# Softmax normalisation folded into the transposes of two attention stages

## The chip, the cores and the metric

The kernel runs on one core of one Trainium2 chip. The metric is the device time of one execution in microseconds (us). The engines named below are TensorE (PE in the profile; PEld is its weight load), VectorE (DVE), ScalarE (ACT), GpSimd (POOL) and SyncE (SP), which issues most of the transfers.

## The reference

The program is a chain of layers on one sequence of 512 positions with 1024 features, in float32: a convolution layer, a linear recurrence, feed-forward layers, and two attention layers. Only the attentions are touched. The first has 4 heads and a causal mask:

```
s = jnp.einsum('bqhd,bkhd->bhqk', qn, k_nope) + jnp.einsum('bqhr,bkr->bhqk', qr, k_rope)
s = s.astype(jnp.float32) * scale
s = jnp.where(k_idx[None, :] <= q_idx[:, None], s, -jnp.inf)
p = jax.nn.softmax(s, axis=-1).astype(v.dtype)
return jnp.einsum('bhqk,bkhd->bqhd', p, v)
```

The second has 8 heads and looks at selected keys only, at most 128 for each query:

```
logits = jnp.einsum('bthd,btkhd->bthk', q_b, k_sel).astype(jnp.float32) * (dh ** -0.5)
logits = jnp.where(valid[:, :, None, :], logits, -jnp.inf)
p = jax.nn.softmax(logits, axis=-1).astype(v.dtype)
return jnp.einsum('bthk,btkhd->bthd', p, v_sel)
```

## The kernel before, in words

Every engine has its own program, and semaphores tie them together; the order on each engine is written out by hand. Queries are worked in four blocks of 128, and query block qb sees (qb+1)*128 keys, so a matrix of probabilities is 128 x 128, 256, 384 or 512.

**First attention** (`attention_pe`, `attention_act`, `attention_dve`): 16 units, one for each of 4 heads and 4 query blocks. For a unit TensorE makes the scores (two instructions of the program, scores and mask, L2342 and L2344). VectorE takes the row maximum (L2407) and scales it (L2409). ScalarE computes exp into SBUF and the row sums beside it (L2391). VectorE takes the reciprocal of the sums (L2418) and multiplies the probabilities by it in place (L2420), which raises `at_norm`. TensorE waits for `at_norm`, then transposes the probabilities, one 128 x 128 block at a time, into PSUM bank 3 of `gp` (L2369). ScalarE copies the result to SBUF (L2384), which raises `at_pt`, and TensorE multiplies by the values (L2351). The loop on TensorE is score(i+2), values(i-1), transposes of i, and then, behind four of the units, a tile of another branch's product (L2563). VectorE weighs that tile (L2951), which lets GpSimd add it up (L2518).

**Second attention** (`pairs_pe`, `pairs_act`, `pairs_dve`): 16 pairs of heads; i//4 is the query block and i%4 the pair. The steps are the same with other lines: scores and mask L3339 and L3342, maximum L3591 and L3592, exp L3564, reciprocal L3599, multiplication L3602 (one for each head), transposes `turn(i, h)` (L3353), copy L3574 or L3579, values L3364. For query blocks 0 and 1 both heads are transposed before one copy; for blocks 2 and 3 the order on TensorE is turn(i, 0), values(i-1), turn(i, 1), and each head has its own copy into SBUF. Beside the pairs TensorE makes products of a convolution (L3305), VectorE selects keys (L3673 to L3698) and ScalarE and GpSimd normalise the convolution (L3505, L3517, L3173 to L3181). The output projection (L3399) comes behind all of it.

Both attentions alternate two buffers of probabilities and two of transposed ones. ScalarE's exp(i) waits until the transposes of i-2 are done.

Of the kernel before, what the change touches and what calls it, by code (L numbers as in the profile page):

```python
# [22 lines left out]
ALU = mybir.AluOpType  # L23
AX = mybir.AxisListType

P = 128
# [185 lines left out]
def build(nc, d, out):  # L212
    ctx = ExitStack()
    with ctx:
# [38 lines left out]
        arena = sb("arena", [P, NT, S])  # L253
# [7 lines left out]
        root = sb("root", [P, S])  # L261
        par = sb("par", [P, NPAR])
        cst = sb("cst", [P, NCST])
        gp = ctx.enter_context(nc.psum_tensor("gp", [P, BANKS, S], F32))
        aux = ctx.enter_context(nc.psum_tensor("aux", [P, BANKS, S], F32))
# [8 lines left out]
        ident, ones, bones = const("ident"), const("ones"), const("bones")  # L274
# [2060 lines left out]
        def attention_pe(pe, A, beside=None):  # L2335
            def score(i):
                u, n = A.units[i], A.u0 + i
                if n >= A.banks:
                    pe.wait_ge(at_exp, n - A.banks + 1)
                if u.chosen:  # L2340
                    pe.wait_ge(sel_ready, u.chosen)
                nc.tensor.matmul(gp[:, n % A.banks, 0:u.nk], u.q, u.k, start=True, stop=False, skip_group_check=True)  # L2342
                lo, m = u.mask
                nc.tensor.matmul(gp[:, n % A.banks, lo:u.nk], A.eye, m, start=False, stop=True,  # L2344
                                 skip_group_check=True).then_inc(at_score, 1)

            def values(i):
                u, n = A.units[i], A.u0 + i
                pe.wait_ge(at_pt, n + 1)
                for b in range(u.nk // P):  # L2350
                    last = nc.tensor.matmul(u.out, u.v(b), A.pt(n)[:, b * P:(b + 1) * P],  # L2351
                                            start=(b == 0), stop=(b == u.nk // P - 1))
                last.then_inc(at_pv, 1)

            score(0)
            score(1)
            if beside:
                beside(-1)
            for i, u in enumerate(A.units):
                n = A.u0 + i  # L2360
                if i + 2 < len(A.units):
                    score(i + 2)
                if i:
                    values(i - 1)
                pe.wait_ge(at_norm, n + 1)
                if n:
                    pe.wait_ge(at_pt, n)
                for b in range(u.nk // P):
                    last = nc.tensor.transpose(gp[:, 3, b * P:(b + 1) * P], A.p(n)[:, b * P:(b + 1) * P], ident)  # L2369
                last.then_inc(at_tr, 1)  # L2370
                if beside:
                    beside(i)
            values(len(A.units) - 1)

        def stat(n, i):
            return root[:, 4 * (n % 2) + i:4 * (n % 2) + i + 1]

        def attention_act(act, A, beside=None):
            def copy(i):
# [23 lines left out]
        def attention_dve(dve, v, A, beside=None):  # L2403
            def maximum(i):
                u, n = A.units[i], A.u0 + i
                dve.wait_ge(at_score, n + 1)
                v(nc.vector.tensor_reduce(stat(n, 0), gp[:, n % A.banks, 0:u.nk], AX.X, ALU.max))  # L2407
                if u.root is None:
                    nc.vector.tensor_scalar(stat(n, 1), stat(n, 0), -A.scale, None, ALU.mult).then_inc(at_max, 1)  # L2409
                else:  # L2410
                    nc.vector.tensor_scalar(stat(n, 1), stat(n, 0), u.root, -1.0, ALU.mult, ALU.mult).then_inc(at_max, 1)

            maximum(0)
            maximum(1)
            for i, u in enumerate(A.units):
                n = A.u0 + i
                dve.wait_ge(at_exp, n + 1)
                v(nc.vector.reciprocal(stat(n, 3), stat(n, 2)))  # L2418
                p = A.p(n)[:, 0:u.nk]
                nc.vector.tensor_scalar(p, p, stat(n, 3), None, ALU.mult).then_inc(at_norm, 1)  # L2420
                if i + 2 < len(A.units):
                    maximum(i + 2)
                if beside:
                    beside(i)
# [655 lines left out]
        score_banks = lambda i: slice(2 * (i % 2), 2 * (i % 2) + 2)  # L3080
        chances = lambda i: 8 + 2 * (i % 2)
        turned = lambda i: (42, 46)[i % 2]
        pair_stat = lambda i, kind: root[:, 8 * (i % 2) + 2 * kind:8 * (i % 2) + 2 * kind + 2]
        head_root = lambda i, n=2, h=0: HST[:, qb_of(i) * 2 * AH + 2 * hp_of(i) + h:qb_of(i) * 2 * AH + 2 * hp_of(i) + h + n]
        head_out = lambda i, h: aux[half(h), qb_of(i) % 2, hp_of(i) * P:(hp_of(i) + 1) * P]
# [244 lines left out]
        def pairs_pe(pe, beside):  # L3330
            def score(i):
                qb, hp, nk = qb_of(i), hp_of(i), nk_of(i)
                lo, chosen = (64, mask3[:, 0, CHUNKED]) if qb == 0 else (0, sel3[:, qb - 1, 0:nk])
                if i >= 2:
                    pe.wait_ge(at_exp, PAIR0 + 2 * (i - 1))
                if qb:
                    pe.wait_ge(sel_ready, qb)
                for h in range(2):
                    nc.tensor.matmul(gp[:, 2 * (i % 2) + h, 0:nk], arena[half(h), dQ + hp, q_cols(qb)],  # L3339
                                     arena[half(h), dK + hp, 0:nk], start=True, stop=False, skip_group_check=True)  # L3340
                for h in range(2):
                    last = nc.tensor.matmul(gp[:, 2 * (i % 2) + h, lo:nk], mask3[:, 0, EYE], chosen, start=False, stop=True,  # L3342
                                            skip_group_check=True)
                last.then_inc(at_score, 1)

            def turn(i, h):
                qb, nk = qb_of(i), nk_of(i)
                at0 = h * nk if qb < 2 else 0
                pe.wait_ge(at_norm, PAIR0 + 2 * i + h + 1)
                if i:  # L3350
                    pe.wait_ge(at_pt, PAIR0 + 2 * i + (0 if qb < 2 else h))
                for b in range(qb + 1):
                    last = nc.tensor.transpose(aux[:, 2, at0 + b * P:at0 + (b + 1) * P],  # L3353
                                               arena[:, chances(i) + h, b * P:(b + 1) * P], ident)
                last.then_inc(at_tr, 1)

            def values(i):
                qb, hp = qb_of(i), hp_of(i)
                pe.wait_ge(at_pt, PAIR0 + 2 * i + 2)
                if qb >= 2 and hp == 0:  # L3360
                    pe.wait_ge(dsa_root, USED + qb - 1)
                for b in range(qb + 1):
                    for h in range(2):
                        last = nc.tensor.matmul(head_out(i, h), arena[:, dV + b, (2 * hp + h) * HD:(2 * hp + h + 1) * HD],  # L3364
                                                arena[:, turned(i) + h, b * P:(b + 1) * P], start=(b == 0), stop=(b == qb),
                                                skip_group_check=True)
                last.then_inc(at_pv, 1)

            score(0)
            score(1)  # L3370
            beside(-1)
            for i in range(PAIRS):
                if i + 2 < PAIRS:
                    score(i + 2)
                turn(i, 0)
                if qb_of(i) < 2:
                    turn(i, 1)
                if i:
                    values(i - 1)
                if qb_of(i) >= 2:  # L3380
                    turn(i, 1)
                beside(i)
            values(PAIRS - 1)
# [204 lines left out]
        def pairs_dve(dve, v, beside):  # L3588
            def maximum(i):
                dve.wait_ge(at_score, PAIR0 + i + 1)  # L3590
                v(nc.vector.tensor_reduce(pair_stat(i, 0), gp[:, score_banks(i), 0:nk_of(i)], AX.X, ALU.max))  # L3591
                nc.vector.scalar_tensor_tensor(out=pair_stat(i, 1), in0=pair_stat(i, 0), scalar=-1.0, in1=head_root(i),  # L3592
                                               op0=ALU.mult, op1=ALU.mult).then_inc(at_max, 1)

            maximum(0)
            maximum(1)
            for i in range(PAIRS):
                dve.wait_ge(at_exp, PAIR0 + 2 * i + 2)
                v(nc.vector.reciprocal(pair_stat(i, 3), pair_stat(i, 2)))  # L3599
                for h in range(2):  # L3600
                    p = arena[:, chances(i) + h, 0:nk_of(i)]
                    nc.vector.tensor_scalar(p, p, pair_stat(i, 3)[:, h:h + 1], None, ALU.mult).then_inc(at_norm, 1)  # L3602
                if i + 2 < PAIRS:
                    maximum(i + 2)
                beside(i)
# [562 lines left out]
```

## Time and profile before

| | us |
|---|---|
| three runs | 3144.32, 3146.17, 3157.05 |
| median | 3146.17 |
| the profiled execution | 3143.76 |
| its span in the trace | 3141.9 |
| TensorE busy, of the span | 3067.1 (98%) |
| VectorE busy | 1595.1 (51%) |
| ScalarE busy | 1177.2 (37%) |
| GpSimd busy | 1276.0 (41%) |

Of the span, the first attention takes from 1975.7 to 2017 us, the second from 2641 to 2717 us. A busy TensorE is not a TensorE at its peak: its instructions are pipelined, and the duration of one includes the time that its result needs to arrive. What one more instruction of a row costs is read from rows that differ in their count.

### The profile page before, as it was taken

To read this page: it belongs to the slowest core of one execution; us is meant where nothing else is said; L and a number is where in the kernel's file an instruction comes from. 1 tells how busy PE (TensorE), PEld (TensorE's weight loads), DVE (VectorE), ACT (ScalarE), POOL (GpSimd) and SP (SyncE) were. 2 spreads that over 40 slices of the span, in tenths; PEclk is the share of its full clock that TensorE was granted. 3 is DMA by queue.
4 is the path that set the end of the run, shared out by engine and by line. 5 is a ranking of instruction groups with operands and counts; after the bars stand their busy time and mean duration, and the time that the engine had idled before them with its cause. 6 is when DMAs were issued, how large, how long until landed. Compare 5 with 4: busy or idle time off the path is not lost.

```text
span 3141.9 us, 58978 instructions
## 1 busy us (share of the span) xinstructions
PE 3067.1 (98%) x23898; PEld 2381.9 (76%) x23898; DVE 1595.1 (51%) x2426; ACT 1177.2 (37%) x1623; POOL 1276.0 (41%) x661
## 2 busy tenths in 40 slices
PE   9999999999999999999999999899999999899999
PEld 6758888868688886888887877678887673458887
DVE  6655555067465554666564641664141776544140
ACT  6413444223444443444334323442232434532221
POOL 4333444434244331444454434344444364224443
PEclk9999999999999999999999999999999999999999
DMA  4212333323100001444553322123333222023333
GB/s 141 80 53 76 99 94 100 103 78 94 48 3 3 3 3 49 141 150 144 188 202 109 97 78 87 39 83 101 94 98 96 67 72 64 13 82 95 100 94 101
DMA packets 74757, 268.64 MB, mean 86 GB/s; under 512 B 8863, under 2 KB 8874, under 8 KB 74384
## 3 DMA queue, kind: packets, MB, share of 16 engines
q1 hardware_dynamic: 73680, 262.53, 26.9%
q0 software_dynamic: 896, 3.52, 0.3%
q8 instruction: 135, 2.21, 0.3%
q14 instruction: 46, 0.38, 0.0%
HBM read 261.71 MB, written 2.10 MB: 84 GB/s over the span
## 4 chain that ended last, share of the span: by engine, by line
PE 88%; issue 6%; DVE 3%; ACT 2%; POOL 1%; DMA 0%; SPq 0%; DVEq 0%; POOLq 0%; ACTq 0%
PE gp L385 66%; PE gp L1344 5%; PE aux L1344 1%; POOL w_low L360 1%; PE gp L2563 1%; PE gp L3282 1%; PE gp L1364 1%; PE aux L1339 1%; PE aux L1480 1%; PE gp L1414 1%; PE aux L3226 1%; PE aux L1443 1%; PE aux L3305 0%; PE aux L808 0%; PE gp L860 0%
## 5 line engine op out<-in xcount | busy, mean ns | idle before, releaser
L360 POOL TENSOR_TENSOR w_low<-ring,w_high 128x1024 fp32r<-128x1024 f32 x413 | 1000.7, 2425 | 1447.1 <-ACT w_high L330 1446.8
L330 ACT ACTIVATE w_high<-ring 128x1024 fp32r<-128x1024 f32 x413 | 437.0, 1059 | 969.6 <-DMA ring<-in_weights 967.3
L385 PE MATMUL gp<-ffn_h,w_high 128*128 128x512 f32 x2432 | 750.3, 390 | 3.0 <-POOL w_low L360 1.3
L385 PEld LDWEIGHTS gp<-ffn_h,w_high 128*128 128x128 f32 x2432 | 455.8, 188 | 101.8 <-issue 3.9
L385 PE MATMUL gp<-ffn_h,w_low 128*128 128x512 f32 x1216 | 473.1, 389 | 0.0
L385 PE MATMUL gp<-ffn_high,w_high 128*128 128x512 f32 x928 | 361.0, 389 | 0.0
L385 PE MATMUL gp<-ffn_low,w_high 128*128 128x512 f32 x864 | 336.1, 389 | 0.0
L385 PE MATMUL gp<-ffn_high,w_low 128*128 128x512 f32 x864 | 336.1, 389 | 0.0
L385 PE MATMUL gp<-in_h,w_high 128*128 128x512 f32 x896 | 278.9, 392 | 0.0
L385 PEld LDWEIGHTS gp<-ffn_h,w_low 128*128 128x128 f32 x1216 | 228.2, 188 | 47.6
L2463 DVE TENSOR_TENSOR arena<-arena 128x512 f32<-128x512 f32 x64 | 102.0, 1593 | 216.8 <-ACTq L164 213.5
L385 PEld LDWEIGHTS gp<-ffn_high,w_high 128*128 128x128 f32 x928 | 174.2, 188 | 36.3
L385 PEld LDWEIGHTS gp<-in_h,w_high 128*128 128x128 f32 x896 | 168.6, 188 | 37.4 <-issue 2.7
L385 PEld LDWEIGHTS gp<-ffn_low,w_high 128*128 128x128 f32 x864 | 162.2, 188 | 33.8
L385 PEld LDWEIGHTS gp<-ffn_high,w_low 128*128 128x128 f32 x864 | 162.2, 188 | 33.4
L385 PE MATMUL gp<-in_h,w_low 128*128 128x512 f32 x448 | 174.6, 390 | 0.0
L385 PE MATMUL gp<-hyena_high,w_high 128*128 128x512 f32 x304 | 121.3, 399 | 1.3 <-POOL w_low L360 1.1
L1173 ACT ACTIVATE arena<-gp,par 128x512 f32<-128x512 f32 x88 | 68.6, 779 | 139.3 <-DVEq L164 139.3
L385 PE MATMUL gp<-hyena_high,w_low 128*128 128x512 f32 x304 | 118.5, 390 | 0.0
L3618 DVE SCALAR_TENSOR_TENSOR X<-gp,par,X 128x512 f32<-128x512 f32 x24 | 18.0, 751 | 186.3 <-PE gp L385 155.9
L2281 DVE TENSOR_TENSOR gp<-gp,arena 128x512 f32<-128x512 f32 x48 | 33.4, 699 | 155.9 <-PE gp L385 154.7
L1205 DVE TENSOR_TENSOR gp<-gp,root 128x512 f32<-128x512 f32 x88 | 61.5, 699 | 81.8 <-PE gp L385 66.2
(598 smaller groups left out, 5052.2 us busy)
## 6 DMA issues: line engine op xcount, KB each, us to landing
ring<-in_weights SPq DMA_DIRECT2D x437, 512.0 KB, 3.6
H<-in_ada SPq DMA_DIRECT2D x48, 512.0 KB, 4.4
arena<-arena SPq DMA_DIRECT2D x32, 67.5 KB, 2.0
X<-in_x SPq DMA_DIRECT2D x4, 512.0 KB, 6.3
out_x<-X SPq DMA_DIRECT2D x8, 256.0 KB, 4.4
arena<-in_sm POOLq DMA_DIRECT2D x1, 1024.0 KB, 5.0
cst<-in_cst SPq DMA_DIRECT2D x1, 756.0 KB, 10.9
arena<-in_hy_f_w POOLq DMA_DIRECT2D x1, 512.0 KB, 5.2
```

The costliest lines, as they stand in the source:

```text
L330: nc.scalar.activation(w_high[:, slab % RING, :], ring[:, slab % RING, :], ACT.Copy).then_inc(high_ready, 1)
L360: nc.gpsimd.tensor_tensor(w_low[:, slab % RING, :], ring[:, slab % RING, :], w_high[:, slab % RING, :], ALU.subtract).then_inc(low_ready, 1)
L385: last = nc.tensor.matmul(gp[:, t.bank, :], wt[:, slab % RING, w], x(k), start=(k == 0 and q == 0), stop=(k == sum(kt) - 1 and q == 2))
L1173: nc.scalar.activation(tmp, z, ACT.Identity, scale=ff_cols(layer, t, 1), bias=pcol("ff_conv_b", layer * 2 * F1T + t.idx)).then_inc(aff_rea ...
L1205: v.go(nc.vector.tensor_tensor(z, z, root[:], ALU.mult))
L1339: last = nc.tensor.matmul(out[h], lhsT[h], rhs[h], start=start, stop=True, skip_group_check=True)
L1344: return nc.tensor.matmul(out[HEADS[cols]], lhsT[HEADS[rows]], rhs[HEADS[rows]], start=start, stop=True, skip_group_check=True)
L1364: last = nc.tensor.matmul(dst, w[:, k, :], X[:, k, :], start=(k == 0), stop=(k == DT - 1))
L1414: last = nc.tensor.matmul(gp[:, t.bank, :], ring[half, slot, i * P:(i + 1) * P], src, start=True, stop=True)
L1443: last = nc.tensor.transpose(aux[:, bank + d, j * P:(j + 1) * P], src(d, j), ident)
L2281: nc.vector.tensor_tensor(z, z, COMB, ALU.mult).then_inc(in2_scaled, 1)
L2463: v(nc.vector.tensor_tensor(f, f, f, ALU.mult))
```

## The change

The probabilities keep the scale that exp gives them. VectorE multiplies the 128 x 128 identity by the reciprocals instead, which makes a diagonal matrix, and TensorE's transpose (the probabilities as the stationary operand, the identity as the moving one) becomes an ordinary float32 product of the same stationary operand with that diagonal matrix. So the result in PSUM is transposed and scaled in one. The diagonal matrices lie in `root` (first attention) and in arena tile 44 (second attention), two buffers for each in turn. The number and the order of the program's instructions on every engine, and all waits, stay as they are.

```diff
@@ attention_pe
                 for b in range(u.nk // P):
-                    last = nc.tensor.transpose(gp[:, 3, b * P:(b + 1) * P], A.p(n)[:, b * P:(b + 1) * P], ident)
+                    last = nc.tensor.matmul(gp[:, 3, b * P:(b + 1) * P], A.p(n)[:, b * P:(b + 1) * P], weight_of(n),
+                                            start=True, stop=True)
...
+        def weight_of(n):
+            return root[:, P * (1 + n % 2):P * (2 + n % 2)]
@@ attention_dve
                 v(nc.vector.reciprocal(stat(n, 3), stat(n, 2)))
-                p = A.p(n)[:, 0:u.nk]
-                nc.vector.tensor_scalar(p, p, stat(n, 3), None, ALU.mult).then_inc(at_norm, 1)
+                nc.vector.tensor_scalar(weight_of(n), ident, stat(n, 3), None, ALU.mult).then_inc(at_norm, 1)
@@ second attention
+        weights_of = lambda i, h: arena[:, 44, (2 * (i % 2) + h) * P:(2 * (i % 2) + h + 1) * P]
...
-                    last = nc.tensor.transpose(aux[:, 2, at0 + b * P:at0 + (b + 1) * P],
-                                               arena[:, chances(i) + h, b * P:(b + 1) * P], ident)
+                    last = nc.tensor.matmul(aux[:, 2, at0 + b * P:at0 + (b + 1) * P],
+                                            arena[:, chances(i) + h, b * P:(b + 1) * P], weights_of(i, h), start=True,
+                                            stop=True)
...
                 for h in range(2):
-                    p = arena[:, chances(i) + h, 0:nk_of(i)]
-                    nc.vector.tensor_scalar(p, p, pair_stat(i, 3)[:, h:h + 1], None, ALU.mult).then_inc(at_norm, 1)
+                    nc.vector.tensor_scalar(weights_of(i, h), ident, pair_stat(i, 3)[:, h:h + 1], None,
+                                            ALU.mult).then_inc(at_norm, 1)
```

## Rows read from the trace of the kernel before

**Rows 1.** The page: TensorE's busy time, and the chain by engine.

```profile
PE 3067.1 (98%) x23898; PEld 2381.9 (76%) x23898; DVE 1595.1 (51%) x2426; ACT 1177.2 (37%) x1623; POOL 1276.0 (41%) x661
PE 88%; issue 6%; DVE 3%; ACT 2%; POOL 1%; DMA 0%; SPq 0%; DVEq 0%; POOLq 0%; ACTq 0%
```

**Rows 2.** Chain of work, first attention: start us, length us, what.

```profile
1977.96 0.33 PE gp L2369
...
2013.96 0.67 PE gp L2369 x4
...
2017.81 7.33 PE gp L2563 x31
```

**Rows 3.** Timeline, end of the second attention: start us, length us, instruction [idle before].

```profile
2714.16 0.60 ACT L3579 ACTIVATE arena<-aux 128x512 f32<-128x512 f32 x1 [0.87 <-PE aux L3353]
2715.71 0.60 ACT L3579 ACTIVATE arena<-aux 128x512 f32<-128x512 f32 x1 [0.95 <-PE aux L3353]
2716.36 1.09 PE L3364 MATMUL aux<-arena 128*64 128x128 f32 x16 [0.69 <-ACT arena L3579]
```

**Rows 4.** Timeline, transposes of 1 and of 3 blocks, first attention.

```profile
1998.81 0.33 PE L2369 MATMUL gp<-cst,arena 128*128 128x128 f32 x1
...
2002.98 0.55 PE L2369 MATMUL gp<-cst,arena 128*128 128x128 f32 x3
```

**Rows 5.** Timeline: four transposes, then four ordinary float32 products of 128 columns.

```profile
2712.03 0.63 PE L3353 MATMUL aux<-cst,arena 128*128 128x128 f32 x4 [1.59 <-ACT arena L3579]
2712.49 1.06 PE L3388 MATMUL aux<-arena,cst 128*128 128x128 f32 x8
```

**Rows 6.** Timeline, VectorE's multiplications undisturbed: pairs of 128, 256, 384, 512 columns.

```profile
2661.62 0.48 DVE L3602 TENSOR_SCALAR arena<-arena,root 128x128 f32<-128x128 f32 x2
2666.04 0.62 DVE L3602 TENSOR_SCALAR arena<-arena,root 128x256 f32<-128x256 f32 x2
2685.35 0.75 DVE L3602 TENSOR_SCALAR arena<-arena,root 128x384 f32<-128x384 f32 x2
2707.99 0.88 DVE L3602 TENSOR_SCALAR arena<-arena,root 128x512 f32<-128x512 f32 x2
```

**Rows 7.** Timeline: VectorE's multiplication beside a GpSimd addition, and what follows.

```profile
1997.26 1.27 POOL L2518 TENSOR_TENSOR H<-H,arena 128x512 f32<-128x512 f32 x1 [5.67 <-DVEq L164]
1997.41 1.21 DVE L2420 TENSOR_SCALAR arena<-arena,root 128x128 f32<-128x128 f32 x1
...
2003.88 1.26 POOL L2518 TENSOR_TENSOR H<-H,arena 128x512 f32<-128x512 f32 x1 [5.35 <-DVEq L164]
2004.03 1.40 DVE L2420 TENSOR_SCALAR arena<-arena,root 128x512 f32<-128x512 f32 x1
...
2005.49 0.66 PE L2369 MATMUL gp<-cst,arena 128*128 128x128 f32 x4 [0.51 <-DVE arena L2420]
...
2012.09 1.81 DVE L2420 TENSOR_SCALAR arena<-arena,root 128x512 f32<-128x512 f32 x1
```

**Rows 8.** Timeline, second attention: a wait for VectorE, and one for ScalarE.

```profile
2661.96 0.69 PE L3353 MATMUL aux<-cst,arena 128*128 128x128 f32 x2 [2.73 <-DVE arena L3602]
...
2694.87 0.52 PE L3353 MATMUL aux<-cst,arena 128*128 128x128 f32 x3 [0.54 <-ACT arena L3579]
```

**Rows 9.** Stretches of the second attention: us, busy of each engine, PEclk, DMA.

```profile
2648.00:2652.00 4.00, 4.00 (x24) 0.89 (x22) 3.83 (x10) 1.87 (x6) 2.54 (x2) 0.57 0.00 0
...
2663.00:2666.00 3.00, 3.00 (x24) 0.76 (x24) 2.86 (x6) 1.25 (x5) 0.00 (x0) 0.62 0.00 0
...
2670.00:2717.00 47.00, 40.83 (x322) 24.34 (x316) 37.66 (x76) 30.31 (x75) 16.80 (x12) 1.00 0.00 1
```

**Rows 10.** Timeline: groups of convolution products at the lower and at the full clock.

```profile
2647.88 4.48 PE L3305 MATMUL aux<-arena 128*32 128x512 f32 x24
...
2653.70 2.78 PE L3305 MATMUL aux<-arena 128*32 128x512 f32 x24
...
2663.21 3.78 PE L3305 MATMUL aux<-arena 128*32 128x512 f32 x24
```

## The prediction

> **What bounds the kernel now.** I read the page first: TensorE is busy 98% of the span and carries 88% of the chain that ended last [rows 1]. So the question for each attention is whether TensorE, or something that TensorE waits for, sets its end. The chain of work answers it for the first attention: it runs from unit to unit through TensorE, with VectorE's multiplication in it where that was late, and its last piece there goes straight on into the products of the next branch [rows 2]. Nothing behind the attention would absorb a delay. In that stretch the chain holds 12 of the 16 groups of transposes, with 1, 3, 4, 2, 3, 4, 1, 2, 4, 1, 2 and 4 blocks, 31 of the 40 blocks; the shown rows are the first and the last of the 12.
>
> For the second attention the printed chain breaks off at a GpSimd operation, so I followed its end in the timeline. The last values product waits for ScalarE's copy of the last head, that copy waits for the transposes of that head, and so on backwards in steps of transposes, copy, transposes, copy [rows 3]. The output projection stands behind the last of them. This is a ping-pong of two engines: a longer piece of either is paid in full.
>
> **The transposes.** The change replaces 40 transposes in the first attention and 80 in the second by float32 products. What does one cost? A group of one transpose lasts 0.33 us and one of three 0.55 [rows 4]: 0.11 us for each more, and 0.22 us that is paid once. Is an ordinary float32 product of the same shape dearer? The trace of before has one just behind a group of transposes: the sum of squares at L3388, 128 x 128 by 128 x 128 in float32. Its source has four products, and the row shows eight instructions and 1.06 us, where four transposes are four instructions and 0.63 us [rows 5]. So a product is two instructions of 0.11 us, and **each block becomes 0.11 us dearer** (0.43 us for four). I take this value, since shape and type are those of the new instruction. TensorE's added work is 120 x 0.11 = 13.2 us in all.
>
> The Trainium skill says it otherwise. Its page "TensorE: Matmul & The Clock Gate", section "Terms", has a transpose mode that is "4× faster for FP32"; by that factor a block would go from 0.11 to 0.44 us. The row of L3388 speaks against that, with a factor of two, and the sum goes by the row.
>
> *How much of it is on the path, first attention.* 31 blocks lie on the chain: 31 x 0.11 = 3.4 us. The other nine (units 1, 4, 10 and 14) stand before waits of TensorE for ScalarE or VectorE; the shortest, behind unit 10, is 0.51 us [rows 7], and the most that one of them adds is 0.33, so I cost them at nothing; if that cover were gone they would be 1.0 us.
>
> *Second attention.* By pairs i, from the timeline:
> - i = 0 and 1, two blocks each, TensorE is the late one: 0.44.
> - i = 3, two blocks behind a wait for VectorE, where two transposes took 0.69 us [rows 8] instead of 0.33 + 0.11 = 0.44, so the clock was low and a further instruction cost about twice: 0.5.
> - i = 4 and 5, four blocks each: 0.9.
> - i = 2, 6 and 7: VectorE, which selects keys there, is the late one: nothing. If not covered, 1.1.
> - i = 8, both heads (each waits for the copy of the other): 0.7.
> - i = 9 and 10, second head only, three blocks: 0.7. The first head's turn is covered by exp and squares on ScalarE. TensorE waits there for ScalarE [rows 8].
> - i = 11 and 12, both heads, since TensorE has no wait between the row at 2694.87 [rows 8] and the second head of i = 12: 0.7 + 0.9.
> - i = 13: the second head 0.4, and of the first half of its 0.4, an estimate, since its copy waited for exp on ScalarE in any case, but the values product behind it on TensorE did not.
> - i = 14, second head, 0.4 (the first is covered by exp); i = 15, both heads, 0.9.
>
> The sum is 0.44 + 0.5 + 0.9 + 0.7 + 0.7 + 1.6 + 0.6 + 0.4 + 0.9 = 6.7 us.
>
> **The multiplications.** VectorE's operation shrinks to 128 columns. Undisturbed, a pair of them takes 0.48, 0.62, 0.75 and 0.88 us for 128, 256, 384 and 512 columns [rows 6]. So the second attention saves 0, 0.14, 0.27 and 0.40 us for each pair, 4 x 0.81 = 3.2 us of VectorE's time; the first, with one head at a time, half of that, 1.6 us. Most of it was not on the path. Three places were. In the second attention pair 7 (0.14) and the first head of pair 8 (0.14) stand in the stretch that VectorE sets: 0.3 us. In the first attention five multiplications on the chain coincided with GpSimd's work, and took 1.2 to 1.8 us [rows 7] instead of the 0.24 to 0.44 of one undisturbed. The row of 128 columns ended 0.09 us after GpSimd's addition did, that of 512 columns 0.29 us after it [rows 7]. VectorE waited for GpSimd to finish, and did its own columns then. The new operation is also SBUF to SBUF in float32, so it will wait as long, and only the part behind the wait shrinks: 0.29 - 0.09 = 0.20 us for 512 columns and nothing for 128. With two of 512 columns, one of 384, one of 256 and one of 128, I take 0.5 us for the five.
>
> No wait, buffer or order changes, so nothing else moves: exp(i) waited for the transposes of i-2 before, and this still guards both the probabilities and the diagonal matrices. Those transposes end 0.11 to 0.44 us later; exp had more room than that, except where ScalarE and TensorE alternate, which is counted above.
>
> **The sum.** 3.4 + 6.7 - 0.5 - 0.3 = +9.3 us. Against the profiled execution, 3143.8 us, that is 3153.1. The three runs of before are 3144.3, 3146.2 and 3157.1, so the profiled execution is 2.4 us below their median; I split that, and take 3145 + 9.3, about **3154 us**, 0.25 to 0.3% above before. A measurement of this kernel can tell about 0.5% (15.7 us) from no change. I expect a real but small loss that stays inside that.
>
> **Rivals.**
> *A. The clock comes back (inside 0.5%).* The granted clock was 0.57 in 2648 to 2652 and 0.62 in 2663 to 2666, between the levels 1.2 and 2.4 GHz, and 1.00 in what follows [rows 9]; before both stretches TensorE had waited for VectorE. There 24 products took 4.48 us where they take 2.78 at the full clock [rows 10], and the same 24 took 3.78 in the second stretch, and the transposes of i = 3 lost 0.25: 1.7 + 1.0 + 0.25, so the low clock costs 3 us. If the denser TensorE kept the clock up, that and half of the 0.5 for i = 3 would come back, and +9.3 would become about +6, 3151 us. Against it: the first low stretch follows a wait that lies ahead of the first replaced transpose and a single pair of blocks. "TensorE: Matmul & The Clock Gate", section "Part 4: PE-mode transpose", says that transposes do not count as busy for the clock as other products do, which would speak for this rival. The trace bears it out poorly: 2670 to 2717 held its full clock with transposes in every pair [rows 9].
>
> *B. VectorE's relief wins (not slower).* It would need VectorE to be what ends every pair. VectorE is busy 37.7 of 47 us in 2670 to 2717 [rows 9], so it is near. At best all of the 4.8 us comes off the path and the transposes hide behind ScalarE in the tail: 6.7 shrinks to about 3, the first attention to 3.4, and the sum is about +1.5, 3147 us. The ping-pong of rows 3 speaks against it.
>
> *C. The product costs four transposes (slower than 0.5%).* If a product with the probabilities as weights took 0.44 us a block, the added 0.33 falls on the same 31 blocks and about 61 in the second attention, and the covers above are too short as well: 92 x 0.33 = 30 us, plus some 3 of lost cover, 3178 us. It decides from 0.2 us a block upwards, since then the sum passes 15.7 us. Against it is the row of L3388.
>
> *D. Every block on the path.* All 120 blocks at 0.11 and no credit for VectorE: +13.2, 3158 us; with one more low stretch of the clock of 2 to 3 us, 3161.
>
> **How the numbers follow.** Forecast (+9.3, within 2 or 3 us): 0.6. A: 0.1. B: 0.08. C: 0.04. D: 0.15. The rest, 0.03, is a mishap of either sign. The range takes in A and D and part of B, and a scatter of the median of 2 or 3 us: 3147 to 3162. For the bound of 0.5%, slower holds C, the end of D and the chance that scatter such as the 3157 of before lands in the median: 0.13. Faster would need -15.7 us, which no case gives: 0.02. Within: 0.85.
>
> **What would show it.** The rows of L2369 and L3353 would carry twice the count (2, 4, 6, 8) and about 0.44, 0.65, 0.87 and 1.06 us. The multiplications would all be 128 columns, 0.24 to 0.29 us undisturbed, and still over 1.1 us where GpSimd works. The first attention, from the first score to the last values product, would be 2.9 us longer, the second 6.4 us. If the group of eight took 1.9 us, C would be right; if PEclk read 1.00 in the first 20 us of the second attention, A; if TensorE still waited for the multiplication in the tail, B. The prediction would be wrong if the time outside both attentions changed.

## The result

| | runs | median us | lowest to highest |
|---|---|---|---|
| before, timed beside it | 22 | 3147.6 | 3138.9 to 3157.7 |
| changed | 22 | 3153.0 | 3146.0 to 3159.3 |

The ratio is 1.0021, with a 95% interval from 1.0012 to 1.0030: the changed kernel is 6.7 us slower, between 3.8 and 9.4. That is inside the half per cent that the prediction called no change, and on the slow side, as it said. The forecast of 3154 us was 1 us off. Its sum of +9.3 us is at the upper end of the interval, and the profiled execution of the changed kernel, at 3159.3 us, was 15.6 us above that of before. Most of what follows is about why one change shows as 6.7 us in a set of runs and as 15.6 us in two profiles, where the prediction had added up 9.3.

The page of the changed kernel, the two rows that answer to [rows 1]:

```profile
PE 3088.4 (98%) x24018; PEld 2402.5 (76%) x24018; DVE 1583.8 (50%) x2426; ACT 1177.5 (37%) x1623; POOL 1274.9 (40%) x661
...
PE 88%; issue 6%; DVE 2%; ACT 2%; POOL 1%; DMA 1%; SPq 0%; DVEq 0%; POOLq 0%; ACTq 0%
```

TensorE has 120 instructions more, one for each block. Here are the products of one, two, three and four blocks in the timeline of the changed kernel's first attention, which answer to [rows 4], and the values product that ends the stage (start us, length us, instruction, idle before):

```profile
2011.51 0.49 PE L2369 MATMUL gp<-root,arena 128*128 128x128 f32 x2
...
2013.21 0.71 PE L2369 MATMUL gp<-root,arena 128*128 128x128 f32 x4
...
2014.98 0.94 PE L2369 MATMUL gp<-root,arena 128*128 128x128 f32 x6
...
2017.85 1.16 PE L2369 MATMUL gp<-root,arena 128*128 128x128 f32 x8 [0.49 <-DVE root L2423]
2019.70 1.09 PE L2351 MATMUL aux<-arena 128*64 128x128 f32 x8 [0.69 <-ACT arena L2388]
```

Each block is two instructions of 0.11 us where it was one. But the group of one block went from 0.33 to 0.49 us and that of four from 0.66 to 1.16: 0.16 and 0.50 us more, not 0.11 and 0.44. The extra 0.05 us comes once in each group. The weight loads show where from: those of the second attention, grouped by line, took 141 ns each in the kernel before and take 194 ns now (140 and 190 ns in the first attention). In a group behind a wait, the first load and the first product start nearly together, and that product takes 0.38 us where the first transpose took 0.33, so it lasts longer by what the load does (line, engine, operation | busy us, mean ns | idle before). First the row of before, then that of the changed kernel:

```profile
L3353 PEld LDWEIGHTS aux<-cst,arena 128*128 128x128 f32 x80 | 9.1, 141 | 12.8 <-DVE arena L3602 6.9 <-issue 4.8
```

```profile
L3357 PEld LDWEIGHTS aux<-arena 128*128 128x128 f32 x160 | 20.6, 194 | 9.5 <-DVE arena L3606 4.7 <-issue 4.5
```

The tail of the second attention is still the ping-pong of [rows 3], with longer steps. From the changed kernel's timeline:

```profile
2728.20 1.13 PE L3357 MATMUL aux<-arena 128*128 128x128 f32 x8
2729.26 1.09 PE L3369 MATMUL aux<-arena 128*64 128x128 f32 x16
2730.28 1.16 PE L3357 MATMUL aux<-arena 128*128 128x128 f32 x8
2732.13 1.09 PE L3369 MATMUL aux<-arena 128*64 128x128 f32 x16 [0.69 <-ACT arena L3584]
```

VectorE's multiplications shrank as forecast, and where GpSimd works they still wait for it. These rows of the changed kernel answer to [rows 7] and [rows 6]:

```profile
1999.70 1.26 POOL L2521 TENSOR_TENSOR H<-H,arena 128x512 f32<-128x512 f32 x1 [6.25 <-DVEq L164]
1999.85 1.20 DVE L2423 TENSOR_SCALAR root<-cst,root 128x128 f32<-128x128 f32 x1
```

```profile
2707.07 0.48 DVE L3606 TENSOR_SCALAR arena<-cst,root 128x128 f32<-128x128 f32 x2
```

**Where the 15.6 us of the two profiles lie.** I measured each stage from the start of its first score to the start of its last values product. The first attention grew from 39.58 to 43.03 us (+3.45), the second from 75.40 to 83.89 (+8.49). The remaining 3.7 us lie outside both, where the code is the same: the changed kernel was 0.94 us late at its first score already, and lost another 2.9 between the attentions. So two profiles do not give the price of the change. The record of the clock in the two traces tells more: 23.9 us at the low clock in the first and 37.7 us in the second, 13.8 us more. Part of the +8.49 is also no work. These are the convolution products behind pair 3, first at the clock of the changed kernel's profile, then the next group at the full clock; before, the same group took 3.78 us [rows 10]:

```profile
2671.46 5.06 PE L3309 MATMUL aux<-arena 128*32 128x512 f32 x24
...
2678.78 2.78 PE L3309 MATMUL aux<-arena 128*32 128x512 f32 x24
```

The table by stretches (us, busy time and count of PE, PEld, DVE, ACT and POOL, then PEclk) has a granted clock of 0.50 to 0.54 there:

```profile
2669.70:2671.50 1.80, 1.80 (x12) 1.25 (x14) 1.73 (x6) 0.48 (x2) 0.00 (x0) 0.50 0.00 0
2671.50:2676.50 5.00, 5.00 (x28) 1.00 (x26) 2.61 (x7) 1.00 (x4) 0.00 (x0) 0.54 0.01 3
```

That is the lower of the two levels, 1.2 of 2.4 GHz, for nearly all of 6.8 us, behind a wait of 2.54 us of TensorE for VectorE. It cost 5.06 - 3.78 = 1.3 us more than in the profile of before. The change isn't needed for it: the profile with only the first attention changed, whose second attention is that of before, has it too:

```profile
2661.50 5.33 PE L3309 MATMUL aux<-arena 128*32 128x512 f32 x24
```

### The profile page after: what moved, and what is told of

Same layout as the page of the kernel before. It is cut to its first block, busy times and chain, and to the rows that moved or that the text cites. A ratio compares the mean times of both kernels' runs of the same rounds, so it can differ in the third digit from the quotient of the medians.

```text
span 3157.5 us, 59218 instructions
## 1 busy us (share of the span) xinstructions
PE 3088.4 (98%) x24018; PEld 2402.5 (76%) x24018; DVE 1583.8 (50%) x2426; ACT 1177.5 (37%) x1623; POOL 1274.9 (40%) x661
## 4 chain that ended last, share of the span: by engine, by line
PE 88%; issue 6%; DVE 2%; ACT 2%; POOL 1%; DMA 1%; SPq 0%; DVEq 0%; POOLq 0%; ACTq 0%
PE gp L385 66%; PE gp L1344 5%; PE aux L1344 1%; POOL w_low L360 1%; PE gp L2566 1%; PE gp L3286 1%; PE aux L1339 1%; PE gp L1364 1%; PE aux L1480 1%; PE gp L1414 1%; PE aux L3230 1%; PE aux L3309 1%; PE aux L1443 1%; PE aux L808 1%; PE gp L860 0%
```

## The experiments

Three theories. **Path:** the products are paid where TensorE or the ping-pong with ScalarE sets the pace, and VectorE's relief is worth under 1 us; the sum of the prediction. **Relief:** the products cost more, and VectorE's shorter operations give several us of it back. **Clock:** much of what separates single profiles is where TensorE's low clock falls.

### TensorE's half alone

```diff
-                    last = nc.tensor.transpose(gp[:, 3, b * P:(b + 1) * P], A.p(n)[:, b * P:(b + 1) * P], ident)
+                    last = nc.tensor.matmul(gp[:, 3, b * P:(b + 1) * P], A.p(n)[:, b * P:(b + 1) * P], ident,
+                                            start=True, stop=True)
```

The same in the second attention; VectorE as before.

> TensorE's half of the change alone: the transposes become float32 products with the identity, and VectorE still multiplies the probabilities in place. Path theory (the product is what costs): first attention +3.9 us over before (39.6 to 43.5 us from the first score to the last values product), second +7.5 at an unchanged clock (75.4 to 82.9), whole kernel +11, ratio 1.0035. Relief theory (VectorE's shorter multiplication pays back several us of the product): more than that, the attentions 3 to 5 us longer than in the changed kernel, ratio 1.004 to 1.005. Clock theory (most of the difference of a single profile is where the low clock falls): the sum of both attentions within 1 us of the changed kernel's once stretches at the low clock are taken out.

Measured: ratio 1.0023 (1.0010 to 1.0036), median 3153.6 us of 12 runs. The first attention took 43.61 us (+4.03), the second 80.82. The last groups of its first attention:

```profile
2017.60 1.16 PE L2369 MATMUL gp<-cst,arena 128*128 128x128 f32 x8 [0.68 <-DVE arena L2421]
2019.44 1.09 PE L2351 MATMUL aux<-arena 128*64 128x128 f32 x8 [0.69 <-ACT arena L2385]
```

The group takes 1.16 us with the identity as with a diagonal matrix, so the price is the product's, not that of another operand. The second attention looks 3 us shorter than in the changed kernel. The cause is the clock, not VectorE: in this profile the products behind pair 3 ran at the full clock.

```profile
2667.37 2.78 PE L3306 MATMUL aux<-arena 128*32 128x512 f32 x24
```

Before had 6.8 us at the low clock in this stage, this profile 3.4, the changed kernel's 10.2. Whole runs were expected at a ratio of 1.0035, which is just inside the interval. Relief, which wanted 3 to 5 us more than the changed kernel, is out: the medians are 3153.6 and 3153.0 us.

### VectorE's half alone

```diff
-                    last = nc.tensor.matmul(gp[:, 3, b * P:(b + 1) * P], A.p(n)[:, b * P:(b + 1) * P], weight_of(n),
-                                            start=True, stop=True)
+                    last = nc.tensor.transpose(gp[:, 3, b * P:(b + 1) * P], A.p(n)[:, b * P:(b + 1) * P], ident)
```

The edit is against the changed kernel, and the same in the second attention.

> VectorE's half alone: it writes the diagonal matrices, but TensorE transposes the unscaled probabilities with the identity as before, so both attentions leave the normalisation out. Path theory: first attention 0.5 us shorter than before, second 0.3 shorter, ratio 0.9997, not to be told from 1. Relief theory: 3 to 5 us shorter in all, ratio 0.9985.

Measured: ratio 0.9997 (0.9982 to 1.0011), first attention 38.98 us (-0.60), second 74.31 (-1.09, with less of it at the low clock than before: PEclk 0.98 against 0.95). The last group of its first attention is a transpose again, at the old price:

```profile
2006.61 0.66 PE L2369 MATMUL gp<-cst,arena 128*128 128x128 f32 x4 [0.60 <-DVE root L2422]
```

The two halves of the first attention add up: +4.03 - 0.60 = +3.43, against 3.45 measured. The 0.60 is also what four multiplications on the chain lost, by its rows: from 1.34, 1.28, 1.42 and 1.82 us to 1.21, 1.21, 1.22 and 1.62.

### One attention at a time

Only the first is changed:

> Only the first attention is changed. Path theory: first attention 43.0 us as in the changed kernel, the second 75.4 as before, whole kernel +3.4, ratio 1.001. Relief theory expects the same length here, so this run tells only where the time lies. If something behind the attention absorbs it: the ratio is 1.000 with the attention longer all the same.

Only the second is changed:

> Only the second attention is changed. Path theory: first attention 39.6, second 82.6 (without a longer stretch at the low clock; 83.9 with one as in the changed kernel), whole kernel +7 to +8.5, ratio 1.0025. If the time behind it absorbs some: the ratio is under 1.0015 with the stage as long.

Measured: with the first alone, ratio 1.0008 (0.9992 to 1.0024), first attention 43.04 us, second 76.92 with unchanged code. With the second alone, ratio 1.0031 (1.0014 to 1.0048), first 39.57, second 83.81. The first attention repeats to 0.1 us wherever its clock stays full. The second does not, and missed the 75.4 us expected of it: 76.92 against 75.40 us for the same instructions. What I found to differ is its time at the low clock, 10.2 us against 6.8 (PEclk 0.93 against 0.95):

```profile
2639.30:2716.20 76.90, 65.81 (x476) 33.60 (x476) 61.15 (x131) 43.70 (x111) 25.70 (x19) 0.93 0.04 14
```

### Every product twice

```diff
                 for b in range(u.nk // P):
-                    last = nc.tensor.matmul(gp[:, 3, b * P:(b + 1) * P], A.p(n)[:, b * P:(b + 1) * P], weight_of(n),
-                                            start=True, stop=True)
+                    for _ in range(2):
+                        last = nc.tensor.matmul(gp[:, 3, b * P:(b + 1) * P], A.p(n)[:, b * P:(b + 1) * P], weight_of(n),
+                                                start=True, stop=True)
```

> The changed kernel with every product of probabilities and diagonal matrix issued twice into the same place: two more instructions of 0.11 us a block, 26 us of TensorE's time, the result the same. Path theory: the blocks that were on the path are so again and the short covers are used up: first attention 43.0 + 31 x 0.22 = 49.8 or up to 51, second 83 + 61 x 0.22 = 96 to 99, kernel +20 to +25 us over the changed one, ratio to before 1.009 to 1.011. If TensorE's time in the attentions is mostly covered: under +12 us over the changed kernel.

Measured: ratio to before 1.0081 (1.0056 to 1.0106), 3175.1 us median of 4 runs, 22 us over the changed kernel's. First attention 50.75 us, second 97.06. Its groups of two and four blocks:

```profile
2016.10 1.16 PE L2370 MATMUL gp<-root,arena 128*128 128x128 f32 x8
...
2021.29 2.05 PE L2370 MATMUL gp<-root,arena 128*128 128x128 f32 x16
```

The stages and the time over the changed kernel lie in the range of the path theory; the ratio is a little under its 1.009 to 1.011, with an interval that reaches into it. The first attention gained 7.72 us over the changed kernel for 80 more instructions of 0.11 us, 8.8 us. That is the worth of 35 of the 40 blocks. The chain now holds 37 of them, all but units 1 and 4, where it held 31 before and 34 in the changed kernel; those that joined paid only for what went beyond their cover. Of 26.4 us added in all some 22 came through. Much of the work that was hidden is hidden by a little only.

### A product of one instruction

```diff
-        weights_of = lambda i, h: arena[:, 44, (2 * (i % 2) + h) * P:(2 * (i % 2) + h + 1) * P]
+        weights_of = lambda i, h: weights3[:, 0, (2 * (i % 2) + h) * P:(2 * (i % 2) + h + 1) * P]
...
-                    nc.scalar.activation(arena[:, chances(i) + h, 0:nk_of(i)], gp[:, 2 * (i % 2) + h, 0:nk_of(i)], ACT.Exp,
+                    nc.scalar.activation(probs3[:, chances(i) - 8 + h, 0:nk_of(i)], gp[:, 2 * (i % 2) + h, 0:nk_of(i)], ACT.Exp,
```

`weights3` and `probs3` are the same places in SBUF, seen as fp32r; the first attention likewise.

 Path theory: both attentions fall back to before's length minus the little that VectorE gives: 39.1 and 75.1 us, ratio 0.9997. If a product costs more than a transpose for another reason than its two instructions: 1 to 4 us longer than before in each attention.

Measured: ratio 1.0012 (0.9997 to 1.0027), first attention 40.82 us, second 78.36. By these figures the expectation, 39.1 and 75.1 us, failed. By the rows it did not: at the full clock a group of four blocks is back at four instructions and 0.56 to 0.63 us.

```profile
2706.82 0.56 PE L3361 MATMUL aux<-weights,probs 128*128 128x128 f32 x4
...
2708.21 0.63 PE L3361 MATMUL aux<-weights,probs 128*128 128x128 f32 x4
```

What was left was the clock: it was low for 3.5 us of the first attention and 14.8 us of the second. The longest stretch ran from the tail of the second attention into the output projection:

```profile
2710.00:2720.00 10.00, 7.50 (x62) 6.74 (x62) 4.92 (x10) 6.37 (x14) 4.95 (x4) 0.80 0.01 2
2720.00:2731.00 11.00, 7.42 (x46) 6.08 (x46) 2.53 (x8) 3.75 (x8) 0.00 (x0) 0.50 0.00 0
```

A second profile of this kernel was to tell whether that is its own doing:

> The fp32r kernel once more, since its first profile had a low stretch of 20.5 us over the end of the second attention and the output projection. If that is this kernel's own (TensorE is too little busy there): again some 20 us at the low clock around the output projection, clock 0.991 or 0.992. If chance: the low stretches are as in the kernel before, clock 0.995 or more, and the whole kernel under 3143 us.

Measured: 3144.9 us, second attention 76.44 us, and no long low stretch over its end (clock 0.995 for the whole run). The time is over the 3143 us that chance was to stay under. So the long stretch does not come every time, but the 12 timed runs of this kernel had more time at the low clock than those of any other (mean clock 0.992; 50 us against 33 before, more than scatter gives). Something in this kernel brings the clock down more often; what, stays open. As it runs, it is not faster than before.

### The same two kernels once more

> The kernel before, once more, for the stretches at the low clock. Clock theory: the low stretches outside the attentions lie elsewhere than in the first profile and move the span by 2 to 6 us, while the first attention stays at 39.6 us within 0.2 and the second at 75.4 minus or plus what the low clock does there.

> The changed kernel once more. Path theory: first attention 43.0 us within 0.2, second 82.6 to 83.9 by the length of the low stretches in it. If the second attention comes out under 80 us, the 83.9 of the first profile was an odd one.

Measured: before, 41.14 and 75.69 us; changed, 43.05 and 83.73. The changed kernel repeats to 0.2 us. Before missed its expectation in the first attention, by 1.56 us, and the clock says why: 0.95 in the stage, where the first profile had 1.00.

```profile
1973.20:2014.30 41.10, 34.72 (x184) 24.29 (x184) 25.59 (x69) 18.93 (x52) 9.08 (x6) 0.95 0.08 26
```

A mean of 0.95 over 41.1 us is about 4 us at half the clock, and it cost 1.56. The two kernels' time outside both attentions scatters as well: 3026.9 and 3032.4 us for before, 3030.6 and 3025.3 for the changed kernel. So the 3.7 us that the first two profiles differ by there can't be laid to the change.

### Filling TensorE's wait ahead of pair 3

```diff
-        QUAD_PAIRS = {-1: (0, 1), 0: (2, 3, 4), 1: (5, 6, 7), 3: (8, 9, 10), 4: (11, 12, 13), 5: (14, 15)}
+        QUAD_PAIRS = {-1: (0, 1), 0: (2, 3, 4), 1: (5,), 2: (6, 7), 3: (8, 9, 10), 4: (11, 12, 13), 5: (14, 15)}
```

Two of the convolution's product groups go behind pair 2 instead of pair 1, so that TensorE works in the 2.5 us in which it waited for VectorE.

> The kernel before, with two of the convolution's product groups (8 instructions of the trace each) moved from behind pair 1 to behind pair 2, into TensorE's wait of 2.7 us for VectorE ahead of pair 3. It tests what the low clock in the second attention hangs on. Clock theory (the wait ahead of pair 3 sets off the low stretch behind it): no low stretch from 2660 to 2670, the second attention 73.5 to 74 us instead of 75.4, at most 1.5 us faster in all. If the wait has nothing to do with it: a low stretch of 3.4 us or more is still there, 75 us.

> The same move on the changed kernel. Clock theory: the 6.8 us low stretch behind pair 3 goes or shortens to nothing, the second attention 80.5 to 81 us instead of 83.8. Otherwise 83 to 84 us.

Measured: on the kernel before, ratio 0.9990 (0.9975 to 1.0005), second attention 74.85 us with PEclk still 0.95. The expectation that the low stretch goes has failed there. It moved: TensorE's wait is now ahead of pair 2, and the products behind that wait, which take 1.92 us at the full clock, ran at a granted clock of 0.57:

```profile
2654.59 0.53 PE L3353 MATMUL aux<-cst,arena 128*128 128x128 f32 x2 [1.44 <-DVE arena L3602]
...
2655.49 3.49 PE L3305 MATMUL aux<-arena 128*32 128x512 f32 x16
```

On the changed kernel the second attention took 81.01 us instead of 83.8, with PEclk 0.98, and the products behind pair 3 ran at full speed behind a shorter wait:

```profile
2664.95 0.71 PE L3357 MATMUL aux<-arena 128*128 128x128 f32 x4 [1.27 <-DVE arena L3606]
2665.96 2.78 PE L3309 MATMUL aux<-arena 128*32 128x512 f32 x24
```

One profile each, one for and one against. Eleven profiles keep the wait of 2.1 to 2.8 us ahead of pair 3, and in ten of them the group behind it took 3.78 to 5.33 us instead of 2.78, with either code; the eleventh, TensorE's half alone, ran it at full speed. So the low clock mostly follows that wait, but that the wait sets it off is not shown.

## One number out of three

Each timed run in the table below lists its mean granted clock. Twice its distance from 1, times the run's length, is the time at the low level. I fitted these 167 runs with a level for each kernel and one common price for low time. (The 22 runs of before in the result's table have no clock on record and are not among them; its 69 runs here were timed beside the other kernels.) The price is 0.43 us for each us at the low clock, and the kernels then differ from before, at equal clock, as below; plus or minus is a 95% interval, 0.03 us for the price.

| kernel | runs | mean us at the low clock | against before, us |
|---|---|---|---|
| before | 69 | 33 | 0 |
| changed | 22 | 28 | +9.7 ± 1.1 |
| TensorE's half | 12 | 30 | +9.0 ± 1.4 |
| VectorE's half | 12 | 25 | -0.8 ± 1.4 |
| first attention | 12 | 29 | +3.1 ± 1.4 |
| second attention | 12 | 37 | +7.4 ± 1.4 |
| every product twice | 4 | 24 | +32.9 ± 2.3 |
| one-instruction product | 12 | 50 | -2.0 ± 1.5 |
| filled wait, on before | 12 | 28 | -1.4 ± 1.4 |

The parts add up (3.1 + 7.4 = 10.5 and 9.0 - 0.8 = 8.2, around 9.7), and they agree with the stages. The two profiles agree too: 13.8 us more at the low clock are 5.9 us at this price, which leaves 9.7 of their 15.6. The same price, as an estimate, takes the low clock out of the second attention. Before it gives 75.40 - 0.43 x 6.8 = 72.5 us, and 72.8 and 72.5 in the two other profiles with unchanged code in that stage. With the products it is 83.89 - 0.43 x 10.2 = 79.5 us, 79.3 and 79.4 in the two others with the whole change there, and 79.4 for TensorE's half. So the second attention costs 6.8 us. No price is needed to see it: two profiles with 10.2 us at the low clock each took 76.92 us without the change and 83.81 with it, 6.9 us apart. With 3.45 for the first, the stages give 10.3, within the interval of the +9.7 of whole runs.

In these sets the plain means of changed and before are 7.3 us apart, and before had 5.6 us more at the low clock, worth 2.4 us: together 9.7. For the 6.7 us of the ratio the same is likely, but not shown, since the 22 runs of before beside it have no clock on record. The clock is recorded to three digits, and one step is 6.3 us at the low level, so a single run can't be corrected, only a set. Whether the denser TensorE keeps its clock up, which was rival A, these runs don't settle. The 5.6 us are known to plus or minus 4.1 and come from sets that were not timed side by side, and the kernel with the shorter VectorE operations, whose TensorE is no denser, had less low time still.

## Why the prediction was right, point by point

- **Path and place.** The chain put 31 of 40 blocks of the first attention on the path, and the stage grew by 3.45 us. The second, followed, was to grow by 6.4 us net and grew by 6.8 at equal clock. Both together were to cost 9.3 us, and cost 9.7 ± 1.1 in whole runs at equal clock. Nothing behind either absorbed it: the output projection started 8.5 us later after its first score, as the last values product did.
- **Price of a product.** Two instructions of 0.11 us, read from the row of L3388 [rows 5]. Right to 0.01 us for each further block. The mis-sized term is what a group pays once: I took 0.22 us before and after, and it is 0.05 us more with a full weight load in front. With 12 groups on the chain that is 0.6 us: 3.4 + 0.6 = 4.0, which is what TensorE's half measured (4.03). In the second attention, where four-block groups behind a wait went from 0.63 to 1.13 us, it is enough for the 0.4 us between 6.4 and 6.8; I haven't split that further. The row of L3388 with eight instructions had no such start, since it followed other work; in the kernel before its twin at 2718.88, behind a wait, takes 1.16 us, so the term could have been read there.
- **Credit for VectorE.** Forecast 0.5 and 0.3 us; VectorE's half measured 0.60 in the first attention. The sum behind the 0.5 had a slip without effect: it counted five multiplications on the chain beside GpSimd's work, and there are four; the one of 128 columns in that state [rows 7] is not on the chain, and was costed at nothing. In the second attention the half gave nothing that can be told from zero (72.8 us at equal clock, against 72.5 to 72.8), so no run shows the 0.3; -0.8 ± 1.4 in all. In the changed kernel the turn of pair 8 no longer waits for VectorE at all, so a shorter multiplication there bought nothing.
- **Covers.** I costed nine blocks of the first attention at nothing. In the changed kernel's chain unit 10's group of three has joined, and VectorE's multiplication for unit 11, shorter by 0.20 us, has left it. The two ways were near equal, since the halves add up to within 0.02 us, so the nine blocks did cost next to nothing. I costed pair 7 at nothing too. The timelines show 0.11 us of its 0.44 passing on to pair 8, whose wait for VectorE had been 0.18 us: the cover was thin. The first head of pair 13, which I guessed at half, 0.2, came with 0.3.
- **The sign of being wrong** was a changed time outside both attentions. The first two profiles have it, by 3.7 us; that time differs by over 5 us between two profiles of one kernel, so with single profiles the sign was too weak to use. Whole runs at equal clock cost no more than the stages do.
- **Rival A** (the clock comes back) has no support in the stage: the group behind pair 3 took 5.06, 5.00 and 4.94 us in the three profiles with the whole change there, but also 5.33 and 5.03 us in two of the profiles with unchanged code, and 2.78 with TensorE's half alone. The low stretch is there with either code. **Rival B** fell with VectorE's half alone. **Rival C** fell with the first row. "TensorE: Matmul & The Clock Gate" of the Trainium skill, section "Terms", has the transpose mode four times faster for float32, and the traces differ from it: a group of four went from 0.66 to 1.16 us, a further block from 0.11 to 0.22, a factor of two. **Rival D** took every block as paid; doubling the products came near to that.
- **Median.** The forecast of 3154 us came within 1 us, partly by luck: the sum was 9.3 where the medians differ by 5.4, and the 3145 us that it was added to, from three runs, lies 2.6 under the median of 22. The two misses cancel.

## What to carry to other kernels

Folding a scale into a transpose trades work on an engine with slack for work on the one that sets the pace, and a float32 product is two instructions where the transpose is one; count blocks on the path times the cost of one more instruction, and add the first weight load of every group. Look for a row of the very shape and type elsewhere in the trace: one row (L3388) gave the price here, and its factor of two held where a factor of four had been in question. Where the effect is a few tenths of a per cent, compare sets of runs at equal clock and stages inside profiles, since single profiles of one kernel differ by as much as the change.

## What the runs showed of the hardware

- A float32 weight load of 128 x 128 took 141 ns for a transpose and 194 ns for a product, on average over the second attention, and a group of products behind a wait paid the difference once.
- An fp32r product of 128 x 128 by 128 x 128 is one instruction and cost what the float32 transpose does, 0.56 to 0.63 us for four.
- A VectorE multiplication from SBUF to SBUF of only 128 columns, 0.29 us alone, took 1.20 us when it started 0.15 us behind a GpSimd addition of 1.26 us, and ended 0.09 us after it: it paid for GpSimd's work, not for its own columns.
- Time at TensorE's low clock cost this kernel 0.43 us per us, and 167 runs of nearly the same program had between about 13 and 70 us of it (clocks from 0.998 to 0.989).
